# Cross attention with cached keys loaded head dimension first, and query norms applied as a scale per token

## What is computed

```python
q = rms_norm((h @ lp['w_xq']).reshape(B, T, X_HEADS, X_DIM), lp['g_xq'])
s = jnp.einsum('bthd,bnhd->bhtn', q, mk).astype(jnp.float32) * (X_DIM ** -0.5)
p = jax.nn.softmax(s, axis=-1).astype(mv.dtype)
o = jnp.einsum('bhtn,bnhd->bthd', p, mv).reshape(B, T, X_HEADS * X_DIM)
return o @ lp['w_xo']
```

## Time and profile before

| | before |
|---|---|
| runs (us) | 1237.33, 1234.31, 1236.36; median 1236.36 |
| profiled execution (us) | 1235.52, of which the profile's span is 1233.7 |
| instructions | 22574 |
| PE busy | 1184.5 us (96%) |
| PEld / DVE / ACT / POOL busy | 1056.4 / 620.8 / 381.0 / 298.4 us |
| mean granted TensorE clock | 0.988 of full speed |
| HBM read / written | 91.12 / 5.25 MB |

### The profile page before, as it was taken

How to read it: one execution, slowest core, us unless ns; L and a number is a source line. 1 busy time by engine, 2 the same in 40 slices (tenths; PEclk the granted TensorE clock), 3 DMA queues, 4 the chain that set the end, 5 groups by cost and what they waited for, 6 DMA issues and landing times.

```text
span 1233.7 us, 22574 instructions
## 1 busy us (share of the span) xinstructions
PE 1184.5 (96%) x8132; PEld 1056.4 (86%) x8132; DVE 620.8 (50%) x1036; ACT 381.0 (31%) x875; POOL 298.4 (24%) x181
## 2 busy tenths in 40 slices
PE   7999999899999999999989977999999999999997
PEld 4799896576989999999867754699999999999997
DVE  0659553876566656666431255444454444444443
ACT  4222024355544444454301246233320002331000
POOL 0126043710566565565702100110000000000000
PEclk9999999989999999999999989999999999999999
DMA  8432102120242222222025222132222222222202
GB/s 336 151 103 91 35 2 61 35 71 9 57 167 76 73 59 52 51 74 73 1 74 199 69 69 69 35 105 84 85 82 81 77 85 86 86 84 73 65 0 77
DMA packets 62629, 97.44 MB, mean 79 GB/s; under 512 B 22961, under 2 KB 41554, under 8 KB 62482
## 3 DMA queue, kind: packets, MB, share of 16 engines
q1 hardware_dynamic: 61970, 94.56, 24.0%
q0 software_dynamic: 576, 1.84, 0.4%
HBM read 91.12 MB, written 5.25 MB: 78 GB/s over the span
## 4 chain that ended last, share of the span: by engine, by line
PE 79%; DVE 5%; issue 4%; POOL 3%; ACT 3%; SPq 3%; DMA 1%; POOLq 0%; DVEq 0%; ACTq 0%
PE bank L1343 33%; PE bank L713 8%; PE bank L775 6%; PE bank L793 4%; PE bank L1144 3%; POOL stat L2615 3%; PE bank L1146 3%; PE bank L1145 3%; PE bank L737 2%; PE bank L1096 2%; PE bank L1172 2%; PE bank L1034 2%; SPq L627 1%; PE bank L1076 1%; PE bank L1054 1%
## 5 line engine op out<-in xcount | busy, mean ns | idle before, releaser
L1343 PE MATMUL bank<-hr,wr 128*128 128x288 f32 x1536 | 205.2, 296 | 1.0 <-DVEq L2292 1.0
L1343 PEld LDWEIGHTS bank<-hr,wr 128*128 128x128 f32 x1536 | 204.9, 189 | 1.4 <-issue 1.4
L1343 PE MATMUL bank<-ur,wr 128*128 128x288 f32 x1536 | 205.3, 296 | 0.0
L1343 PEld LDWEIGHTS bank<-ur,wr 128*128 128x128 f32 x1536 | 205.0, 189 | 0.1
L2615 POOL TENSOR_TENSOR stat<-stat,cst 128x32 f32<-128x32 f32 x32 | 173.7, 5428 | 2.5
L1144 PE MATMUL bank<-wq_high,c_parts 128*128 128x288 f32 x512 | 162.3, 317 | 3.5 <-ACT hT L1651 2.5
L1146 PE MATMUL bank<-wq_low,c_parts 128*128 128x288 f32 x512 | 151.5, 296 | 0.0
L1145 PE MATMUL bank<-wq_high,c_parts 128*128 128x288 f32 x512 | 150.6, 294 | 0.0
L2401 DVE CAST wr<-ring 128x1024 fp32r<-128x1024 f32 x64 | 44.4, 694 | 209.3 <-PE bank L1343 208.6
L2184 DVE TENSOR_REDUCE stat<-hT 128x8 f32<-128x512 f32 x128 | 86.9, 684 | 78.2 <-ACT hT L1651 74.2
L1144 PEld LDWEIGHTS bank<-wq_high,c_parts 128*128 128x128 f32 x512 | 96.5, 188 | 8.2 <-ACT hT L1651 3.9
(11 more groups left out here) (392 smaller groups left out, 1878.1 us busy)
## 6 DMA issues: line engine op xcount, KB each, us to landing
ring<-in_ring_w_dram SPq DMA_DIRECT2D x106, 512.0 KB, 3.5
arena<-in_cache_ckv_dram SPq DMA_DIRECT2D x128, 128.0 KB, 2.0
arena<-in_cache_mk_dram SPq DMA_DIRECT2D x8, 512.0 KB, 3.4
arena<-in_cache_mv_dram SPq DMA_DIRECT2D x8, 512.0 KB, 9.2
mixT<-in_x_dram SPq DMA_DIRECT2D x1, 2048.0 KB, 12.6
arena<-in_cache_kpe_dram SPq DMA_DIRECT2D x128, 16.0 KB, 1.6
out_dram<-hT SPq DMA_DIRECT2D x4, 512.0 KB, 3.2
mixT<-in_w_qb_dram SPq DMA_DIRECT2D x1, 1152.0 KB, 5.8
```

Source lines behind the costliest of these rows:

```text
L1343: ins = mm(outs[c][:, 0:HALF], w[:, ew, k, :], src[:, ex, k0 + k, c * HALF:(c + 1) * HALF], start=(start and k == 0 and n == 0), stop=(sto ...
```

## The change

- The host hands the cached memory keys over with the head dimension on the partitions (`mk_t`). SP loads a sequence's 512 KB straight into `kmcT`, which has four buffers now; four loads go out ahead of the values, and the loads of sequences 4 to 7 wait until the scores of the sequence four before are done. The 64 transposes and both sets of copies are gone.
- The query projection is evacuated by VectorE with the gain multiplied in, and squared by ScalarE from PSUM. TensorE sums the squares with the squares as the stationary operand and 8 columns of ones, so a token's sum stands on the token's partition: 8 such matmuls for heads 0 and 1 behind the third head's projection, and for heads 2 and 3 in the loop's second step, with 8 more for samples. ScalarE and VectorE compute the roots on 8 or 10 columns. The queries stay unscaled; the negated maxima are multiplied by the root, and the exponential gets the root as its scale.
- In the MLA stage the key norms' root goes from POOL to ScalarE (Ln, Exp) and VectorE (Newton step), the multiply of the keys moves from the second to the fourth turn of VectorE's loop, key heads 4 to 7 are turned before 0 to 3, ScalarE waits for the state only before heads 0 to 3, absorbed(1) and the padded queries move ahead of the last turned queries, and TensorE waits for each turned query only before it reads it.

The diff, cut to its core and with the indentation that a hunk shares left out:

```diff
@@ -81,9 +81,9 @@
 TURNED_ORDER = (
-    *(("kT", h) for h in range(4)), ("vp", 0), "qTs", *(("kT", h) for h in range(4, MH)), ("vp", 1), ("qabs", 0),
-    ("qT", 0), ("qT", 1), ("vp", 2), ("qT", 2), ("qT", 3), ("qT", 4), ("qT", 5), ("vp", 3), ("qT", 6), ("qT", 7),
-    ("qabs", 1), "qpd")
+    *(("kT", h) for h in range(4, MH)), ("vp", 0), "qTs", *(("kT", h) for h in range(4)), ("vp", 1), ("qabs", 0),
+    ("qT", 0), ("qT", 1), ("vp", 2), ("qabs", 1), ("qT", 2), ("qT", 3), ("qT", 4), ("qT", 5), "qpd", ("vp", 3),
+    ("qT", 6), ("qT", 7))
 def make_plan():
@@ -204,18 +204,15 @@
-for j in range(XH + 1):
+for j in range(XH):
     for c in range(2):
-        if j < XH:
-            turn(("xq", j, c))
-    for c in range(2):
-        if j:
-            turn(("ms_xq", j - 1, c))
+        turn(("xq", j, c))
+    if j == 2:
+        turn(("ms_xq", 0))
+fill(("ms_xq", 1), 0)
...
     fill(("cp", n % 4, n // 4), 3 + n % 2)
-    for m in range(2):
-        fill(("ck", n, m), 5 + m)
@@ -344,6 +341,8 @@
 gxq = stat[:, 600:601]
+m_xq = [stat[:, 96:104], stat[:, 104:114]]
+r_xq = [stat[:, 116:124], stat[:, 124:134]]
@@ -426,15 +425,14 @@
 vmc = view(arena, 0, NB, 2, XH * XD)
-kmc = view(arena, 8192, 2, 2, XH * XD)
-kmcT = view(arena, 10240, 2, 2, XH, P)
+kmcT = view(arena, 8192, 4, 2, XH, P)
...
 acc = r_ff = rstd[:, :]
-ACC_FF = 2 * (KD - 1) + XH - 1
+ACC_FF = 2 * (KD - 1) + XH
@@ -657,20 +655,27 @@
 sp.wait_ge(S("phase_end"), MET[4])
-mk = cache_mk[0].rearrange("b (n p) h d -> b p n (h d)", p=P)
 mv = cache_mv[0].rearrange("b (n p) h d -> b p n (h d)", p=P)
-for b in range(2):
-    sp.dma_start(kmc[:, b, :, :], mk[b]).then_inc(S(f"kmc_in{b}"), 16)
+def load_cached_keys(b):
+    sp.dma_start(kmcT[:, b % 4, :, :, :].rearrange("p m h c -> p (m h c)"), mk_t[b]).then_inc(
+        S(f"kmc_in{b % 4}"), 16)
+for b in range(4):
+    load_cached_keys(b)
...
     load_tile(n)
-for b in range(2, NB):
-    bk, c = PLAN[("ck", b - 2, 1)]
-    sp.wait_ge(bank_full[bk], c)
-    sp.dma_start(kmc[:, b % 2, :, :], mk[b]).then_inc(S(f"kmc_in{b % 2}"), 16)
+for b in range(4, NB):
+    if b % 2 == 0:
+        sp.wait_ge(S("kmcT_used"), b // 2 - 1)
+    else:
+        bk, c = PLAN[("css", b // 2 - 2)]
+        sp.wait_ge(bank_full[bk], c)
+    load_cached_keys(b)
@@ -1008,19 +1013,19 @@
 value_rows(2)
+absorbed(1)
...
     turned_queries(h)
-value_rows(3)
-for h in range(6, MH):
-    turned_queries(h)
-absorbed(1)
...
 filled(ins, "qpd")
+value_rows(3)
+for h in range(6, MH):
+    turned_queries(h)
 arrive(pe)
-for key in [("kT", h) for h in range(MH)] + [("vp", t) for t in range(4)] + [("qT", h) for h in range(MH)]:
+for key in [("kT", h) for h in range(MH)] + [("vp", t) for t in range(4)]:
@@ -1204,69 +1212,59 @@
     project(("wo", j), lambda k: ring[:, s, k, :], mixT, KD)
-for j in range(XH + 1):
-    if j < XH:
-        s = slot(pe, W_XQ + j)
-        project(("xq", j), lambda k: ring[:, s, k, :], hTk, KD, name=None if j else "x")
-    if 0 < j < XH:
-        pe.wait_ge(S("acc"), KD - 1 + j)
-        for c in range(2):
-            o = reopen(pe, ("ms_xq", j - 1, c))
-            filled(mm(o[:, 0:HALF], ones, mixT[:, j - 1, c * HALF:(c + 1) * HALF], start=True, stop=True),
-                   ("ms_xq", j - 1, c))
-    if j == XH:
-        outs = [reopen(pe, ("ms_xq", j - 1, c)) for c in range(2)]
-        for c in range(2):
-            mm(outs[c][:, 0:HALF], ones, acc[:, c * HALF:(c + 1) * HALF], start=True, stop=False)
-        pe.wait_ge(S("sq_xq"), j)
-        for c in range(2):
-            filled(mm(outs[c][:, 0:HALF], ones, mixT[:, j - 1, c * HALF:(c + 1) * HALF],
-                      start=False, stop=True), ("ms_xq", j - 1, c))
+def query_squares(u):
+    pe.wait_ge(S("acc"), KD - 1 + 2 * u + 2)
+    o = reopen(pe, ("ms_xq", u))
+    for t in range(4):
+        for e in range(2):
+            n = 2 * t + e
+            ins = mm(o[:, 8 * n:8 * n + 8], mixT[:, 2 * u + e, t * P:(t + 1) * P], ones[:, 0:8],
+                     start=True, stop=True)
+    if u:
+        for g in range(2):
+            for h in range(XH):
+                ins = mm(o[32 * h:32 * h + 32, 64 + 8 * g:72 + 8 * g],
+                         mixT[:, h, TP + 32 * g:TP + 32 * g + 32], ones[:, 0:8], start=True, stop=True)
+    filled(ins, ("ms_xq", u))
+for j in range(XH):
+    s = slot(pe, W_XQ + j)
+    project(("xq", j), lambda k: ring[:, s, k, :], hTk, KD, name=None if j else "x")
+    if j == 2:
+        query_squares(0)
...
-def cached_keys(b):
-    pe.wait_ge(S(f"kmc_in{b % 2}"), 16 * (b // 2 + 1))
-    for m in range(2):
-        o = reopen(pe, ("ck", b, m))
-        for h in range(XH):
-            ins = tr(o[:, h * P:(h + 1) * P], kmc[:, b % 2, m, h * XD:(h + 1) * XD], ident)
-        filled(ins, ("ck", b, m))
 def sample_scores(q):
-    pe.wait_ge(S("xq"), XH)
-    for m in range(2):
-        pe.wait_ge(S(f"kmcT{m}"), q + 1)
+    pe.wait_ge(S("xq"), 2 * XH)
+    pe.wait_ge(S(f"kmc_in{q % 4}"), 16 * (q // 4 + 1))
...
         ins = mm(o[32 * h:32 * h + 32, (q % 2) * NM:(q % 2 + 1) * NM], xqT[:, h, c0:c0 + 32],
-                 kmcT[:, q % 2, :, h, :], start=True, stop=True)
+                 kmcT[:, q % 4, :, h, :], start=True, stop=True)
...
-cached_keys(0)
-cached_keys(1)
...
         t, u = pairs[n]
-        pe.wait_ge(S("xq"), 2 * u + 2)
+        pe.wait_ge(S("xq"), 4 * u + 4)
...
         filled(ins, ("cs", t, u))
+    if n == 1:
+        query_squares(1)
...
         sample_scores(n - 3)
-    if 3 <= n <= NB:
-        cached_keys(n - 1)
@@ -1554,6 +1552,10 @@
     freed(nc.scalar.copy(qf[0:m, t, c * 384:(c + 1) * 384], o[0:m, 0:384]), ("qf", t, c))
+if n == 0:
+    act.wait_ge(S("ss_mla"), TILES + 1)
+    link(A(stat[:, 232:272], stat[:, 192:232], ACT.Ln))
+    A(stat[:, 232:272], stat[:, 232:272], ACT.Exp, scale=-0.5).then_inc(S("root"), 1)
@@ -1580,9 +1582,8 @@
-act.wait_ge(S("state_in"), 32)
 act.wait_ge(S("gon"), 5)
-for h in range(4):
+for h in range(4, MH):
@@ -1590,21 +1591,22 @@
 act.nop().then_inc(S("qTs"), 1)
-for h in range(4, MH):
+act.wait_ge(S("state_in"), 32)
+for h in range(4):
...
 turned_queries(4)
-value_rows(3)
-turned_queries(6)
...
                    o[r, :].rearrange("p (h b t) -> p h b t", h=MH, b=NB)).then_inc(S("qpd"), 1)
+value_rows(3)
+turned_queries(6)
@@ -1699,31 +1701,27 @@
        scale=(EPS * XD / D) ** 0.5).then_inc(S("squares"), 1)
- for j in range(XH + 1):
-     if j < XH:
-         for c in range(2):
-             o = full(act, ("xq", j, c))
-             freed(nc.scalar.copy(xqT[:, j, c * HALF:(c + 1) * HALF], o[:, 0:HALF]), ("xq", j, c))
-         for c in range(2):
-             b, n = PLAN[("xq", j, c)]
-             act.wait_ge(bank_free[b], n)
-         A(mixT[:, j, :], xqT[:, j, :], ACT.Square).then_inc(S("sq_xq"), 1)
-     if j:
-         for c in range(2):
-             first_root(("ms_xq", j - 1, c), mixT[:, 3 + j, c * HALF:(c + 1) * HALF], XD, eps=eps2)
+ for j in range(XH):
+     for c in range(2):
+         o = full(act, ("xq", j, c))
+         act.wait_ge(S("xq"), 2 * j + c + 1)
+         A(mixT[:, j, c * HALF:(c + 1) * HALF], o[:, 0:HALF], ACT.Square).then_inc(S("sq_xq"), 1)
+         act.wait_ge(S("sq_xq"), 2 * j + c + 1)
+         act.nop().then_inc(bank_free[PLAN[("xq", j, c)][0]], 1)
+ def query_roots(u):
+     o = full(act, ("ms_xq", u))
+     m, r = m_xq[u], r_xq[u]
+     n = m.shape[1]
+     link(A(m, o[:, 0:8 * n].rearrange("p (n r) -> p n r", r=8)[:, :, 0], ACT.Identity, bias=eps2,
+            scale=1.0 / XD))
+     act.nop().then_inc(bank_free[PLAN[("ms_xq", u)][0]], 1)
+     link(A(r, m, ACT.Ln))
+     A(r, r, ACT.Exp, scale=-0.5).then_inc(S("root"), 1)
+ query_roots(0)
  pairs = [(t, u) for u in range(2) for t in range(4)]
...
 def sample_exponentials(u):
@@ -1731,7 +1729,7 @@
 A(psx[:, 2 * u + e, :], o[:, e * NM:(e + 1) * NM], ACT.Exp,
-  bias=stat[:, 64 + 2 * u + e:65 + 2 * u + e],
+  bias=stat[:, 64 + 2 * u + e:65 + 2 * u + e], scale=r_xq[1][:, 8 + u // 2:9 + u // 2],
@@ -1754,12 +1750,12 @@
         A(pcx[:, n % 2, e, :], o[:, e * NM:(e + 1) * NM], ACT.Exp,
-          bias=stat[:, 2 * n + e:2 * n + e + 1],
+          bias=stat[:, 2 * n + e:2 * n + e + 1], scale=r_xq[u][:, 2 * t + e:2 * t + e + 1],
...
     act.nop().then_inc(bank_free[PLAN[("cs", t, u)][0]], 1)
-if 3 <= n <= NB:
-    cached_keys(n - 1)
+if n == 1:
+    query_roots(1)
@@ -2047,6 +2043,7 @@
 dve.wait_ge(S("ss_mla"), TILES)
+V.tensor_scalar(stat[:, 192:232], stat[:, 192:232], 1.0, MV * EPS, ALU.mult, ALU.add).then_inc(S("ss_mla"), 1)
 def states(u):
@@ -2079,18 +2076,24 @@
         S("ss_mla"), 1)
 for n, t in enumerate(QUERY_ORDER):
     if n == 1:
-        dve.wait_ge(S("r_mla"), 3)
+        dve.wait_ge(S("root"), roots["k"] + 1)
+        m, r = stat[:, 192:232], stat[:, 232:272]
+        link(V.scalar_tensor_tensor(out=m, in0=m, scalar=-0.5, in1=r, op0=ALU.mult, op1=ALU.mult))
+        link(V.tensor_tensor(m, m, r, ALU.mult))
+        link(V.scalar_tensor_tensor(out=r, in0=m, scalar=1.5, in1=r, op0=ALU.add, op1=ALU.mult))
```

(58 more changed lines are left out.)

53 lines of the change are left out of this document (19 added, 34 removed).

## The result

The changed kernel takes 1220.5 us, the median of four runs (1217.4 to 1220.8), against 1236.8 of the kernel before on the same chip (1234.3 to 1239.3): a ratio of 0.986, interval 0.985 to 0.988 (ratios here come from all runs of both kernels, so they differ a little from the quotient of the medians). The forecast was 1216.0, with 1209 to 1223. The profiled execution took 1220.8 against 1235.5.

The account below looks back on a forecast made before the run. TensorE, busy 96%, was held by a state DMA in MLA turning and a repeated round in cross attention; gains of 4.0 + 16.4 = 20.4 us from 1235.5 gave 1215.1, or 1216 as a median, range 1209 to 1223.

Parts of the forecast that it names:

- place one: Turning of MLA keys and queries: first score at 251.0 instead of 255.0, 4.0 us gained, bounds 2.0 and 5.0.
- place two: Cross attention: 16.4 us gained, from 10.3 before the rounds, 5.0 in them and 1.1 after; bounds 12.4 and 18.
- What bounds the kernel: TensorE busy 96% of the span; a state DMA delays MLA key turning, a repeated round chains the cross attention.
- the ring of the turned cached keys: Cross attention: exponentials, key copy, key transposes and probability transposes repeat every 3.57 us; without copies and key transposes it is gone.
- What follows it: After the last rotary multiply, TensorE has 9.5 us from 241.1, ending at 250.6, then 0.4 before the first score.
- a sign that its sum was wrong: Cross attention: first exponentials later than 722, or rounds above 3 us, would prove the sum wrong.
- the head: Cross attention up to the first exponentials: first at 723.4, second at 724.6 instead of 734.95, 10.3 us earlier.
- The rounds: Cross attention: six rounds at 2.5 us, bound by VectorE and ScalarE together, take 15.6 instead of 20.6, gaining 5.0.
- The tail: Cross attention, last exponential to sample values: 9.0 instead of 10.1 without key copies, gaining 1.1 us.
- Place one gives nothing: Turning of MLA keys and queries: a wait on POOL or VectorE's late copy replaces the DMA's; 1220, chance 0.08.
- The rival of the clock: Cross attention: TensorE's clock falls and stays low, costing 23.4 us, or 1270 with the output projection slowed; chance 0.03.
- the fall at 726 goes away: Cross attention: TensorE's clock, granted 0.50 between 726 and 728 before, would stay at full rate through the rounds.

Follow-up runs that it names:

- e5: The changed kernel with cached keys as before: old layout, two buffers, transposed and copied in the loop; 1230.6 us (ratio 0.995).
- e4: The changed kernel with three idle matmuls of 512 columns, results overwritten, in TensorE's wait for the last query tile; 1218.1 us (ratio 0.986).
- e1: The changed kernel with the turning of MLA keys and queries as before the change, only the cross attention changed; 1220.8 us (ratio 0.989).
- e6: The changed kernel with the sample scores of the four pairs of sequences on four banks instead of two; 1216.7 us (ratio 0.985).
- e7: The changed kernel with the 24 cross attention exponentials scaled by the constant 0.01 instead of each query's root; 1217.3 us (ratio 0.985).
- e8: The changed kernel with two value blocks moved ahead of the query wait and four banks for the sample scores; 1214.9 us (ratio 0.982).
- e10: The changed kernel with two buffers of cached keys instead of four; 1217.9 us (ratio 0.986).
- e2: The kernel before with only the turning of MLA keys and queries changed, the cross attention as before; 1234.1 us (ratio 0.998).

## Why the prediction was right, and where it was off

The forecast, faster to 1216, came 4.5 us short, inside the range. Between the two profiled executions the gain was 14.7 us of the 20.4 summed: 3.0 are missing in place one and 1.8 in place two, and the other stretches took 0.9. Over the traces of the same code place one misses about 2 and place two 0.4 to 3.1. Step by step:

**What bounds the kernel**: right. No DMA is in the chain at place one, and e5 shows the ring of the turned cached keys.

**Place one, when work is ready**: right. The last rotary multiply ends at 241.8; predicted 241.1, in a trace that runs 0.5 later. **What follows it**: wrong by size. "From there it has 9.5 us" at full clock, and 0.4 before the first score. e4, without the fall of the clock, has 10.0 us of work and 0.98 of gap, 1.1 more than I gave. The changed kernel has 13.76 between the same points (241.82 to 255.58), where e4 has 11.01: 2.75 us of clock (1.5 to 2.75 over the six traces). So 22.54 us was predicted from the first key transpose to the first score, and 26.64 came: 0.2 late, 1.1 for work and gap, 2.75 for the clock. 1.05 of that came back in the prompt attention, which lost the lower level it ran at before (0.57 over 254 to 262). The step that failed was to carry full-clock durations across an idle stretch that the prediction itself had written down as 3 us long. Its own rows held the warning: behind the wait of 3.35 us eight transposes took 1.94, where sixteen took 1.91 without a wait. With the value block behind them the kernel before paid some 1.5 us there, and the predicted sum returned that without naming it.

The prediction had named a sign that its sum was wrong, first exponentials later than 722. They came at 723.38. Place two began 3.9 us later than predicted, 3.0 of it because place one gave 1.0 instead of 4.0 and 0.9 in stretches that hold no edit.

**Place two, the head**: right to 0.1 us from the first query projection, at the first two pairs of exponentials. Sixteen passes of the sums took 1.78 us from start to start (722.45 to 724.23; I gave 1.7), and the second set 2.09 to its end (2.4). ScalarE's small functions took 0.21 to 0.27 each (0.25). VectorE's small steps took 0.16 to 0.18, on the side of the earlier trace rows, and the samples' multiply 0.23.

**The rounds**: the sum came out (15.4 against 15.6), in part by luck. In e1 and e6, where the clock stayed up, the same six rounds took 14.0 us; the fall at 726 made up the rest. ScalarE alone is the bound from the fourth pair on, not ScalarE and VectorE together; in the two rounds before it, ScalarE waits for maxima of late scores. A round is 2.08 us without sample exponentials and 3.4 with them, not 2.5 throughout. The bound "the scale pointer could make an exponential dearer" was true, 0.09 us each, 0.85 by the last pair and 1.8 in the whole end part (e7 against e1).

**The tail**: wrong. "9.0: 1.1" was a subtraction of copies from the old 10.1, and 10.9 came: from the last pair of exponentials at 740.08 to the values at 750.96. The copies' place is taken by a wait for the samples' bank (2.44): with four banks the same piece takes 9.3 (e6, e8). The lower clock from 744 (windows at 0.50) costs nothing there, since e4, back at full clock by 746.6, idles 1.57 us and starts its values after the same 10.9. Taking the bank away uncovers VectorE's columns.

**Transfers**: nothing was charged and nothing was due. The cover I named, ten microseconds by four buffers, wasn't needed: in e10 two loads come late by up to 1.13 us and the total is the same.

**Rivals.** "Place one gives nothing" named 1220, and 1220.5 came, but place two had its part in that. It was half true by the sum (2 us of 4), though not by its mechanism: a wait of 3.15 us on POOL did take the place of the 3.35, but the prediction had counted it, at 3.0; what it hadn't counted was the clock behind it. The rival of the clock was sought in place two and as a fall that stays. It fell there too, but came back within a few microseconds each time:

```profile
724.00:726.00 2.00, 1.76 (x23) 1.48 (x23) 1.00 (x3) 1.79 (x7) 0.00 (x0) 0.81 0.00 0
726.00:728.00 2.00, 2.00 (x8) 1.66 (x7) 1.53 (x4) 1.37 (x6) 0.00 (x0) 0.50 0.00 0
728.00:730.00 2.00, 2.00 (x16) 1.00 (x15) 1.12 (x4) 1.11 (x3) 0.00 (x0) 0.83 0.00 0
```

So "the fall at 726 goes away" was wrong here. Of the nine traces with the new place two and its new key layout the clock fell there in six and stayed at 1.00 in three (e1, e6, e7), behind the same idling before the scores (1.42 us) and the same small matmuls. The changed kernel and e1 have the same code there and differ, so the code alone doesn't decide it; what does stays open. The Trainium skill, "TensorE: Matmul & The Clock Gate", on the HAM clock gate, says that the monitor runs free of the kernel, so that the number of slow matmuls at a kernel's start varies from run to run. The traces show the like behind a wait in mid-kernel: behind the same wait of 3.15 us the value block took 3.62 us in the changed kernel and 2.69 in e2.

## What to carry to other kernels

Where a plan leaves TensorE idle for some microseconds, charge the idle time and then ask what runs right behind it: here 3.15 us of waiting cost another 1.5 to 2.75 in the work that followed, and the order that filled the hole got both back. Look for the engine that has no gaps in the loop before sizing a resource: two more buffers of keys changed nothing, while of 0.09 us on each of 24 exponentials 1.8 came through. Take more than one trace of the same code before reading a difference of 1 or 2 us: where the clock falls can make as much. Don't get a tail by subtracting what was removed; lay out once more who waits for whom there.

## What the runs showed of the hardware

- Six passes of 512 columns that compute nothing, 2.84 us in a wait, made the kernel's stretch 1.6 to 3.4 us shorter (e4 against six traces).
- A TensorE wait of 3.13 to 3.15 us was followed by work at a granted clock of 0.50 in all six traces that have it, and one of 1.42 us with many small matmuls behind it in six of nine.
- A scale read from memory for each partition, on an exponential of 128x256 that already reads its bias so: 0.56 us against 0.47 with a constant scale.
- Sums of squares with 8 columns of ones cost 0.11 us a pass with 128 stationary columns (16 in 1.78, start to start) and some 0.02 with 32 (16 in 0.31).
- The 512 KB of a cached batch landed in 4.0 us (median) with each partition's keys in one piece, and in 3.4 before; in e10 it was 3.3 and in e6 3.4. The new layout brought no faster transfer.
